# Running sums of a depthwise convolution moved from SBUF to PSUM banks

## The reference, cut to what matters

```python
conv_x = conformer_conv(cu_x, conv_dw_w, conv_dw_b, conv_ln_w, conv_ln_b, w_conv_out)   # GLU, 31 taps, layernorm, silu
h_x, h_c = mlstm_bidirectional(...)                                                    # gates from mg, queries, keys, values
q_x = apply_rope(attn_heads(aq_x, ATTN_HEADS, q_norm_w), cos, sin)                     # 8 query heads of 64, 2 key/value heads

def dwconv(x, w, b):          # centred depthwise convolution over positions, w (31, 512)
    y = lax.conv_general_dilated(x, w[:, None, :], window_strides=(1,), padding=((15, 15),), feature_group_count=512)
    return y + b

def apply_rope(x, cos, sin):  # x1, x2: halves of a head
    return concatenate([x1 * c - x2 * s, x1 * s + x2 * c], axis=-1)
```

## Time and profile before

| what | value |
|---|---|
| median of three executions | 3082.34 us |
| the profiled execution: its time, its span | 3079.21 us, 3077.3 us |
| mean granted TensorE clock | 0.959 |
| PE busy | 2844.6 us (92%) |
| DVE busy | 1436.6 us (47%) |
| ACT busy | 1356.5 us (44%) |
| POOL busy | 1535.9 us (50%), 624 instructions of L919 |

### The profile page before, as it was taken

The page is one execution under the profiler, slowest core; times in us unless marked ns, Lnnn a source line. Parts: engine busy times, 40 slices in busy tenths (PEclk is TensorE's granted clock), DMA queues, the critical chain, the costliest instruction groups (busy, mean ns, idle before and its releaser), DMA issues.

```text
span 3077.3 us, 44386 instructions
## 1 busy us (share of the span) xinstructions
PE 2844.6 (92%) x18070; PEld 2444.8 (79%) x18070; DVE 1436.6 (47%) x2113; ACT 1356.5 (44%) x2178; POOL 1535.9 (50%) x628
## 2 busy tenths in 40 slices
PE   7999999889999979789999989899998899998999
PEld 6889799788879968656777767688887768888899
DVE  5665411457541147953443432432336945445543
ACT  5464544446454443344333323443334444434555
POOL 4667578556757845311232324344444524345687
PEclk8999999999999989889999999899998889999999
DMA  5457765435777522201111212222223212233454
GB/s 185 130 191 241 240 226 192 130 112 185 257 247 228 177 96 89 68 29 35 55 62 55 76 55 96 74 98 96 95 98 103 71 60 94 78 103 112 143 183 160
DMA packets 144879, 386.60 MB, mean 126 GB/s; under 512 B 11824, under 2 KB 64304, under 8 KB 144688
## 3 DMA queue, kind: packets, MB, share of 16 engines
q1 hardware_dynamic: 144688, 383.87, 37.9%
HBM read 382.77 MB, written 1.05 MB: 125 GB/s over the span
## 4 chain that ended last, share of the span: by engine, by line
issue 36%; POOL 30%; PE 26%; DVE 6%; ACT 1%; POOLq 0%; DMA 0%; SPq 0%; DVEq 0%; ACTq 0%
POOL w_lo L919 30%; PE bank L960 7%; PE bank L961 7%; PE bank L962 7%; DVE cy L2086 3%; PE bank L1300 1%; PE bank L993 1%; DVE sd L1704 1%; PE bank L1270 1%; PE bank L1222 1%; PE bank L1237 1%; POOLq L918 0%; PE bank L1019 0%; PE bank L1228 0%; DVE work L2001 0%
## 5 line engine op out<-in xcount | busy, mean ns | idle before, releaser
L919 POOL TENSOR_TENSOR w_lo<-raw,w_hi 128x1024 fp32r<-128x1024 f32 x624 | 1535.7, 2468 | 1530.2 <-ACT w_hi L1331 1529.3
L960 PE MATMUL bank<-h_hi,w_hi 128*128 128x256 f32 (+1 forms) x3456 | 1132.0, 328 | 75.8 <-DVE h_lo L2007 31.7
L961 PE MATMUL bank<-h_lo,w_hi 128*128 128x256 f32 (+1 forms) x3456 | 1103.0, 319 | 0.0
L962 PE MATMUL bank<-h_hi,w_lo 128*128 128x256 f32 (+1 forms) x3456 | 1101.7, 319 | 0.0
L960 PEld LDWEIGHTS bank<-h_hi,w_hi 128*128 128x128 f32 x3456 | 673.5, 195 | 171.9 <-issue 57.6
L1331 ACT ACTIVATE w_hi<-raw 128x1024 fp32r<-128x1024 f32 x624 | 654.8, 1053 | 311.1 <-PE bank L962 203.1
L961 PEld LDWEIGHTS bank<-h_lo,w_hi 128*128 128x128 f32 x3456 | 675.9, 196 | 42.7 <-issue 3.1
L962 PEld LDWEIGHTS bank<-h_hi,w_lo 128*128 128x128 f32 x3456 | 674.2, 195 | 41.4
L960 PE MATMUL bank<-hid_hi,w_hi 128*128 128x256 f32 (+1 forms) x704 | 218.2, 310 | 0.0
L961 PE MATMUL bank<-hid_lo,w_hi 128*128 128x256 f32 (+1 forms) x704 | 217.9, 309 | 0.0
L962 PE MATMUL bank<-hid_hi,w_lo 128*128 128x256 f32 (+1 forms) x704 | 217.9, 309 | 0.0
(11 more groups left out here) (270 smaller groups left out, 3566.0 us busy)
## 6 DMA issues: line engine op xcount, KB each, us to landing
raw<-stream SPq DMA_DIRECT2D x624, 512.0 KB, 3.4
spare_lo<-stream SPq DMA_DIRECT2D x32, 512.0 KB, 5.5
mix<-stream SPq DMA_DIRECT2D x32, 512.0 KB, 6.2
spare_hi<-stream SPq DMA_DIRECT2D x32, 512.0 KB, 5.6
xs<-x_rows SPq DMA_DIRECT2D x4, 256.0 KB, 4.5
xs<-ctx_rows SPq DMA_DIRECT2D x1, 1024.0 KB, 14.9
out_rows<-xs SPq DMA_DIRECT2D x8, 128.0 KB, 2.3
cst<-consts SPq DMA_DIRECT2D x1, 896.5 KB, 11.2
```

Source lines behind the costliest of these rows:

```text
L919: nc.gpsimd.tensor_tensor(w_lo[:, unit % SPLIT, :], raw[:, unit % RAW, :], w_hi[:, unit % SPLIT, :], ALU.subtract).then_inc(lo_ready, 1)
L960: nc.tensor.matmul(acc, wh, x_hi[:, k, c0:c1], start=k == 0, stop=False)
L961: nc.tensor.matmul(acc, wh, x_lo[:, k, c0:c1], start=False, stop=False)
L962: last = nc.tensor.matmul(acc, wl, x_hi[:, k, c0:c1], start=False, stop=k == t.k - 1)
```

## The change

- The running sums of both convolution tiles go to `X[2]` and `X[3]`. Only the last of the 31 taps writes `cy`.
- To free these banks, the transposes of the values go from `X[2]` to `X[1]`, those of the gates from `X[3]` to columns 64 to 127 of `X[4]`.
- The query rotation used `X[0]` and `X[1]` in turn, now `X[0]` alone, so from the second rotation on PE waits for the previous one's `aq_ready`, where it waited for the one before that.
- The product with the sine is written over the rotated tile in PSUM, and the SBUF buffer `a_rot` is gone.

```diff
-                        if i >= 2:
-                            pe.wait_ge(aq_ready, (AG + 1) * l + i - 1)
-                        nc.tensor.matmul(X[i % 2][:, 0:SEQ], c_("rot_att"), aq[:, i, SEQ:T2], start=True, stop=True)\
+                        if i:
+                            pe.wait_ge(aq_ready, (AG + 1) * l + i)
+                        nc.tensor.matmul(X[0][:, 0:SEQ], c_("rot_att"), aq[:, i, SEQ:T2], start=True, stop=True)\
                             .then_inc(aq_rot, 1)
...
-                            last = nc.tensor.transpose(X[2][:, t * P:(t + 1) * P], av_t[:, t * P:(t + 1) * P], ident)
+                            last = nc.tensor.transpose(X[1][:, t * P:(t + 1) * P], av_t[:, t * P:(t + 1) * P], ident)
...
-                            last = nc.tensor.transpose(X[3][:, t * 16:(t + 1) * 16], mg_t[:, t * P:(t + 1) * P],
+                            last = nc.tensor.transpose(X[4][:, (4 + t) * 16:(5 + t) * 16], mg_t[:, t * P:(t + 1) * P],
...
-                                y = by_stream(cy[:, pair + j, cols])
+                                y = by_stream(X[2 + j][:, cols])
+                                out = y if tap < CONV_K - 1 else by_stream(cy[:, pair + j, cols])
                                 z = z2[:, j, first:2, tap:tap + SEQ]
                                 w = v_("conv_dw_w_2", l, 4 * tap + pair + j)
                                 if tap == 0:
                                     C.do(V.tensor_scalar(y, z, w, v_("conv_dw_b_2", l, pair + j), MUL, ADD))
                                 else:
                                     C.settle(tapped[j])
-                                    C.do(V.scalar_tensor_tensor(y, z, w, y, MUL, ADD))
+                                    C.do(V.scalar_tensor_tensor(out, z, w, y, MUL, ADD))
...
-                        C.do(V.tensor_tensor(a_rot[:, :], X[i % 2][:, 0:SEQ], c_("sin_ax"), MUL))
+                        turned = X[0][:, 0:SEQ]
+                        C.do(V.tensor_tensor(turned, turned, c_("sin_ax"), MUL))
                         C.do(V.tensor_tensor(x, x, c_("cos_ax"), MUL))
                         C.settle()
-                        V.tensor_tensor(x, x, a_rot[:, :], ADD).then_inc(aq_ready, 1)
+                        V.tensor_tensor(x, x, turned, ADD).then_inc(aq_ready, 1)
```

More of the change, by code:

```diff
@@ L689, in mixer_stack_kernel @@
     a_sq = e.put("a_sq", [P, T2])
-    a_rot = e.put("a_rot", [P, SEQ])
     e = u.view()
@@ L1591, in _ @@
                         E.need(av_turned)
-                        nc.scalar.activation(av[:, :, :], X[2][:, :].rearrange("p (t n) -> p t n", n=P), ACT.Copy)\
+                        nc.scalar.activation(av[:, :, :], X[1][:, :].rearrange("p (t n) -> p t n", n=P), ACT.Copy)\
                             .then_inc(av_out, 1)
@@ L2108, in _ @@
                         E.need(mg_turned)
-                        V.tensor_tensor(pre[:, :, :], X[3][:, 0:64].rearrange("p (t g) -> p t g", g=16),
+                        V.tensor_tensor(pre[:, :, :], X[4][:, 64:128].rearrange("p (t g) -> p t g", g=16),
                                         v_("mlstm_gate_b_2", l, 0, 16).unsqueeze(1).to_broadcast([P, 4, 16]), ADD)\
```

## The result

The changed kernel has a median of 3037.47 us (3030.99 to 3041.79, four runs) against 3082.3 us (3079.41 to 3083.29, four runs) before: a ratio of 0.9859, with a 95% interval of 0.9844 to 0.9874. The forecast was 3040.3 us, in a range of 3030 to 3058. The profiled execution took 3041.79 us, with a span of 3039.9.

A forecast was written before the change was run, and what follows sets the result against it. DVE was taken to bound two stretches, some 155 us together, with PE's own work as the floor. Layer 0's 25 and layer 1's 17 us make 42 off 3082.3: 3040.3 us, range 3030 to 3058.

The forecast's parts named there:

- The mechanism: In the convolution taps, a DVE instruction with two SBUF inputs waits for POOL; long taps are up to 2.2 us longer.
- The cost of a PSUM tap: Taps in both layers: 0.671 and 0.404 us from start to start, or up to 0.08 more; the low end was taken.
- Layer 0: First glu to first score: 25 us sooner, between 21 and 27.4, with PE deciding over DVE's chain.
- The 9.7 us: Layer 0, second pair's stage: PE's work falls from 64.5 to 54.8 us when its clock stays full.
- The term for hits: Layer 0: POOL delays L2095 and L2103, five each; ten at 45% and 1.2 us make 5.4 us.
- Layer 1: The stage gets 17 us shorter, at least 10.5 and 20.9 at most.
- PE's floor: Layer 1, PE's own work from 2402 us: 46.2 us busy becomes 39.9, or 41.7 with small gaps and a wait.
- scores at 1297 and 2428: Sign of a right forecast: the first attention scores of layers 0 and 1 start at about these times in us.
- C: Attention steps, or denser POOL hits on L2095 and L2103, give back half of 42 us: 3061 us; chance 0.10.
- D: Taps reading and writing one bank take two cycles a column: 39 us slower, 3121 us; chance 0.02.
- E: Long taps come from something other than the inputs' place, or the clock falls: about nothing changes, 3082 us; chance 0.05.
- B: PSUM taps don't overlap, 0.75 and 0.48 us each: 32 us off, 3050 us, or 3057 with hits; chance 0.13.

The follow-up runs named there:

- the two kernels with the memset: The kernels before and after the change, with POOL filling w_lo by a memset instead of subtracting: 2978.86 and 2980.02 us.
- layout_only: The changed kernel with the running sums back in SBUF: 3077.65 us, ratio 0.9991 to the kernel before.
- second_pair: The changed kernel with only the second pair of channel tiles summed in PSUM, the first in SBUF: 3067.72 us, ratio 0.9956 to the kernel before.
- in_sbuf_out_psum: The changed kernel with taps 1 to 29 reading both inputs from SBUF and writing PSUM: 3074.14 us, ratio 0.9989 to the kernel before.
- first_pair: The changed kernel with only the first pair of channel tiles summed in PSUM, the second in SBUF: 3049.17 us, ratio 0.9900 to the kernel before.

## Why the prediction was right

**The mechanism** (two SBUF inputs against POOL) was read from the spread of single lines: L2279 with one input in PSUM against L2086 and L2103. The two kernels that move only an input or only the output, and the two without POOL's reads, show it.

**The cost of a PSUM tap.** I bounded it by 0.671 from below and 0.75 from above, and took the low end. Measured: 38.28/58 = 0.660, and in layer 1 22.81/58 = 0.393. That is below the bound only because 0.671 and 0.404 are tenths of a short row of ten, whose last tap counts with its whole duration. Rows of equal length compare so: ten taps 6.71 us before and 6.66 to 6.68 after, sixty 39.83 and 39.58 (the two kernels with the memset). A tap in PSUM is 3 to 5 ns shorter. The table of the Trainium skill (page VectorE: DVE Perf Modes, section The TRN2 errata) would put 65 ns on top, an estimate from its cycles for SBUF and for PSUM sources; the trace disagrees for this operation. The first tap of a tile, a `tensor_scalar`, did get longer, from 542 to 798 ns, where I had 0.7 us.

**Layer 0.** DVE's first reciprocal was to follow ACT's root: it does, after an idle time of 8.46 us. The first score was to come 25 us sooner within the stage, with PE as the bound; it came 162.3 - 136.5 = 25.8 sooner, and PE's clock was 1.00 as assumed. The 9.7 us that the full clock was to take off PE's work were 9.3: from the first rotation to `gsum` PE is busy 64.5 us before and 55.2 after. The term for hits on the ten instructions with two SBUF inputs was 5.4 us; the mean of L2104 is 798 ns in this stage, 1.9 us too much for five, one scaling was 0.24 too long, and L2116, which I hadn't counted, 1.8: 4.0 us.

**Layer 1.** 17 forecast, 114.8 - 99.3 = 15.5 measured. PE's wait of 10.5 us went as said. PE's floor was sized wrongly, though. I took 8.4 us as what the clock was short of full and put three quarters of it, 6.3, on PE's work. Two windows of the kernel before, and the same work after the change, show another split:

```profile
2402.00:2412.40 10.40, 0.00 (x0) 0.00 (x0) 10.30 (x13) 0.18 (x1) 7.79 (x2) 0.61 0.29 92
2412.40:2461.80 49.40, 46.17 (x288) 41.52 (x288) 48.95 (x78) 25.55 (x35) 21.78 (x8) 0.91 0.21 69
...
2383.00:2429.10 46.10, 43.31 (x289) 39.37 (x287) 40.74 (x75) 25.62 (x36) 19.04 (x8) 0.96 0.28 88
```

The lowest clock, 0.61, fell on the 10.4 us in which PE stood still, and costs nothing there. That is 4.1 of the 8.4 us; on the work lay 46.2 x 0.09 = 4.2. PE's work went from 46.2 us to 43.3, by 2.9, and not to 39.9. So of the 20.9 us that I had as the most, 2.1 were never there. A part of the rest is in the hits:

```profile
L2095 DVE SCALAR_TENSOR_TENSOR aq<-aq,vec,sd 128x256 f32<-128x256 f32 x2 | 4.7, 2356 | 0.1
L2104 DVE TENSOR_TENSOR aq<-aq,cst 128x256 f32<-128x256 f32 x5 | 4.2, 843 | 0.0
```

Two scalings take 2.1 and 2.6 us in place of 0.5. The first has room. The second, with a product of 1.45 us ahead of it, delays `aq_scaled` and gives PE its wait of 2.0 us, and the clock is 0.89 in the 16 us around it. I had taken 17 with 3.9 us for such hits; that it came so near to 15.5 is in part luck, since the too large floor stood under it.

**The rest.** 25.8 + 15.5 = 41.3 us; the ratio says 43 (3082.3 x 0.0141), with an interval of 39 to 48. Nothing is given back that these runs can tell from none: PE's waits in the attention steps of layer 0 are the same 15.7 us in 13 times before and after. From the first score of layer 0 to the first `glu` of layer 1 the changed kernel's trace has 1035.7 us against 1032.8, and behind the first score of layer 1 604.8 against 607.8. The first of these stretches lies between 1030 and 1036 us in all the runs, on the average 2 us longer where all sums lie in PSUM (1034.5 against 1032.4), and the second some 2 us shorter there; one makes up for the other. The absolute times that were to show it (scores at 1297 and 2428) are 1300.1 and 2435.1 in this trace, which was 4 us late from the start, and 1293.7 and 2428.7 in the second run of the changed kernel. Rivals C, D and E are out, and so is B, by the spacing. (In D, 279 ns for 256 columns is 1.09 ns a column, not 1.05.)

**Where the working was wrong**, though the sum was not: PE's floor in layer 1, as above, and what PE cuts off. I thought, in the expectations too, that PE cuts the sum off only when both pairs are in PSUM. It cuts off the second pair's gain already when that pair is changed alone, and nothing of the first pair's; so the two add in layer 0.

## What to carry to other kernels

Suspect that GpSimd blocks VectorE where a VectorE line has a clean median and a maximum about one GpSimd instruction higher; look at how many of the line's inputs lie in SBUF, and if there are free PSUM banks, keep a running value there. Sum up what such hits cost on the chain that sets the stage, and then look at the floor of the next engine, here PE's work at full clock, since it decides how much arrives. When PE's gaps go, count the time that it worked at the lower clock after them too: in layer 0 that was 9.3 of 25.8 us. But split such a window where PE stands still: a low clock there costs nothing.

## What was not expected of the hardware

- VectorE can also keep GpSimd out, and for much longer than one instruction. In the kernel before, one subtraction took 14.82 us, beside 32 taps in a row of which none was longer than 492 ns. PE did not wait for its result, but stood waiting for the scaled query from 2402 us on:

```profile
2392.53 14.82 POOL L919 TENSOR_TENSOR w_lo<-raw,w_hi 128x1024 fp32r<-128x1024 f32 x1 [5.49 <-ACT w_hi L1331]
```

  The same subtraction takes 14.8 us in each of the traces of layout_only, second_pair and in_sbuf_out_psum, where the first pair's taps have two SBUF inputs, and 3.5 us is the longest in layer 1 of first_pair. After the change the longest is 3.56 us. The Trainium skill (page SBUF — State Buffer, section SBUF: two separate sides) describes a lock for one whole instruction, for whichever of the two starts first; with VectorE issuing such instructions back to back, the row shows GpSimd kept out over many. What decides whether a tap or the subtraction is the one kept waiting, these runs don't show.
- Without POOL's reads the kernel is another 57 us faster than the changed one (by the two ratios, 0.9859 and 0.9673). The first `glu` starts at 1127.0 us there, at 1163.6 us in the changed kernel and at 1157.2 in its second run, so more than half of it lies in the first block, where no tap is. How much of it is contention and how much the shorter POOL instruction, these runs don't tell apart.
